# A decoder layer step on one core: stores a tile later, a strip loaded in four pieces and first, eight copies for sixteen, squares before a split

## What is computed

```python
q, k, v, u = mixer_inputs(rmsnorm(xp, norm_mix_g[l]), w_in[l])
att = dilated_attention_prompt(q, k, v, rpb_table)      # 12 heads of 64, causal, strided keys
u_full = jnp.pad(u, ((0, 0), (CONV_K - 1, 0), (0, 0)))
xp = xp + mixer_outputs(att, u_full, conv_w[l], conv_b[l], conv_ln_g[l], conv_ln_b[l], w_out[l])
...
xp = xp + cross_attend(rmsnorm(xp, norm_x_g[l]), mk, mv, w_xq[l], w_xo[l])
xp = xp + swiglu(rmsnorm(xp, norm_ffn_g[l]), w_ffn_gate[l], w_ffn_up[l], w_ffn_down[l])
...
kc = jnp.concatenate([cache_win_k[l].astype(k.dtype), k], axis=1)   # samples: 2048 cached + 8 new
s_wk.append(kc[:, -buf_len:])                                       # the cache moved on by 8 rows
```

## Time and profile before

| what | us |
|---|---|
| median of 3 runs | 1956.98 (1952.81 to 1958.29) |
| profiled execution, whole | 1964.15 |
| its span, first to last instruction | 1962.4 |
| TensorE busy | 1891.4 |
| DVE busy | 1030.5 |
| POOL busy | 513.6 |
| ACT busy | 442.4 |

### The profile page before, as it was taken

One profiled execution on the slowest core, in us unless ns is written; L12 is line 12 of the kernel. 1 busy time (PEld: TensorE's weight loads), 2 busy tenths in 40 slices (PEclk: granted clock), 3 DMA queues, 4 the chain that ended last, 5 costly groups with the idle time before them and its releaser, 6 DMA issues.

```text
span 1962.4 us, 33021 instructions
## 1 busy us (share of the span) xinstructions
PE 1891.4 (96%) x13253; PEld 1757.0 (90%) x13253; DVE 1030.5 (53%) x2099; ACT 442.4 (23%) x902; POOL 513.6 (26%) x380
## 2 busy tenths in 40 slices
PE   6999999999999899999999999999999999999998
PEld 6999888666666799999658999999999999999997
DVE  6698726666666553511653374544544544544544
ACT  5100013555545521200441031001001001001005
POOL 2332222000010135353001223222332222222234
PEclk9999999999999999899999999999999999999998
DMA  5399976686767512223630123432432432411102
GB/s 154 125 318 316 334 237 187 190 245 204 203 215 251 178 44 76 65 84 110 222 111 22 43 78 137 171 128 85 170 128 85 170 128 87 175 46 43 43 32 92
DMA packets 220002, 281.36 MB, mean 143 GB/s; under 512 B 7521, under 2 KB 206569, under 8 KB 218153
## 3 DMA queue, kind: packets, MB, share of 16 engines
q1 hardware_dynamic: 219901, 279.94, 43.8%
HBM read 266.48 MB, written 113.89 MB: 194 GB/s over the span
## 4 chain that ended last, share of the span: by engine, by line
PE 81%; DVE 8%; ACT 3%; SPq 3%; DMA 3%; issue 1%; POOL 1%; DVEq 0%; POOLq 0%; ACTq 0%
PE bank L1558 26%; PE bank L1594 13%; PE bank L1325 8%; PE bank L1086 7%; PE bank L1342 5%; PE bank L1033 3%; PE bank L1204 2%; DVE sp L2193 2%; PE bank L1305 2%; DMA w_raw<-in_w_in_dram 2%; SPq L651 2%; ACT p_T L1723 2%; PE bank L1177 2%; PE bank L1187 1%; PE bank L1520 1%; PE bank L1232 1%
## 5 line engine op out<-in xcount | busy, mean ns | idle before, releaser
L924 POOL CAST w_hi<-w_raw 128x1024 fp32r<-128x1024 f32 x98 | 105.1, 1073 | 967.7 <-issue 325.6
L1558 PE MATMUL bank<-g_lo,w_hi 128*128 128x362 f32 (+1 forms) x1008 | 334.0, 331 | 0.0
L1558 PE MATMUL bank<-g_hi,w_lo 128*128 128x362 f32 (+1 forms) x1008 | 333.6, 331 | 0.0
L1558 PE MATMUL bank<-g_hi,w_hi 128*128 128x362 f32 (+1 forms) x1008 | 331.0, 328 | 0.0
L926 POOL TENSOR_TENSOR w_lo<-w_raw,w_hi 128x1024 fp32r<-128x1024 f32 x98 | 248.2, 2533 | 7.8
L2599 DVE TENSOR_TENSOR xT<-bank,xT 128x362 f32<-128x362 f32 (+1 forms) x264 | 141.3, 535 | 121.7 <-PE bank L1594 121.7
L1558 PEld LDWEIGHTS bank<-g_hi,w_lo 128*128 128x128 f32 x1008 | 191.3, 190 | 0.0
L1558 PEld LDWEIGHTS bank<-g_hi,w_hi 128*128 128x128 f32 x1008 | 189.8, 188 | 0.3 <-POOL w_lo L926 0.3
L1558 PEld LDWEIGHTS bank<-g_lo,w_hi 128*128 128x128 f32 x1008 | 189.6, 188 | 0.0
L1594 PE MATMUL bank<-act_lo,w_hi 128*128 128x362 f32 (+1 forms) x480 | 157.5, 328 | 0.0
L1594 PE MATMUL bank<-act_hi,w_hi 128*128 128x362 f32 (+1 forms) x480 | 157.5, 328 | 0.0
(11 more groups left out here) (303 smaller groups left out, 3844.9 us busy)
## 6 DMA issues: line engine op xcount, KB each, us to landing
out_sk_dram<-in_cache_win_k_dram SPq DMA_DIRECT2D x24, 2040.0 KB
out_sv_dram<-in_cache_win_v_dram SPq DMA_DIRECT2D x24, 2040.0 KB
kb<-in_cache_win_k_dram SPq DMA_DIRECT2D x48, 512.0 KB, 5.0
vn<-in_cache_win_v_dram SPq DMA_DIRECT2D x22, 1024.0 KB, 8.2
w_raw<-in_w_in_dram SPq DMA_DIRECT2D x22, 512.0 KB, 11.9
w_raw<-in_w_ffn_gate_dram SPq DMA_DIRECT2D x22, 512.0 KB, 3.8
w_raw<-in_w_ffn_up_dram SPq DMA_DIRECT2D x22, 512.0 KB, 3.8
w_raw<-in_w_ffn_down_dram SPq DMA_DIRECT2D x22, 512.0 KB, 3.7
```

What stands on the lines that cost most here:

```text
L924: pool.tensor_copy(w_hi[slot][:, :], w_raw[slot][:, :]).then_inc(w_hi_done, 1)
L1558: last = pe.matmul(out, w, r, start=start, stop=stop)
```

## The change

Four parts, none of which changes what is computed.

1. In SP's loop the K of pair c is stored in the turn of tile 10 + 3c and V in that of tile 11 + 3c, a tile later than before. The store of K of pair 4 then comes behind the loop.
2. `d_strip` is loaded by four DMAs of 16 rows in place of eight of 8 rows. The first of these loads, with the wait for `d_made` ahead of it, is issued before `strip` and the last K store, not behind them.
3. `new_rows` fills `d_new` with eight copies, not sixteen: three units' columns are written by one copy from a broadcast source.
4. The last chunk's squares and their addition come ahead of the third group's `g_hi` and `g_lo`.

```diff
-                c, which = divmod(n - FIRST_QKV - 5, 3)
-                if n >= FIRST_QKV + 5 and which < 2:
+                c, which = divmod(n - FIRST_QKV - 6, 3)
+                if n >= FIRST_QKV + 6 and which < 2:
                     (store_k, store_v)[which](c)
                 for part in copies[:2]:
                     keep_rows(*part)
                 del copies[:2]
+            store_k(4)
...
             def load_sample_strip(p):
                 for g in range(4):
-                    for hh in range(2):
-                        row, head = 32 * g + NI * hh, 2 * member(4 * p, g)[0] + hh
-                        sp_.dma_start(d_strip[row:row + NI, :],
-                                      bass.AP(tensor=A["g_scratch"].tensor, offset=head * GL + ZERO - 7,
-                                              ap=[[1, NI], [1, BUF + NI]])).then_inc(d_loaded, 16)
+                    c = member(4 * p, g)[0]
+                    sp_.dma_start(d_strip[32 * g:32 * g + 2 * NI, :],
+                                  bass.AP(tensor=A["g_scratch"].tensor, offset=2 * c * GL + ZERO - 7,
+                                          ap=[[GL, 2], [1, NI], [1, BUF + NI]])).then_inc(d_loaded, 16)
...
             load_keys(0, 0)
+            sp_.wait_ge(d_made, 1)
+            load_sample_strip(0)
             load_strips(0)
             store_k(5)
-            sp_.wait_ge(d_made, 1)
-            load_sample_strip(0)
             sp_.wait_ge(k_out, 96)
...
-                pool.wait_ge(d_loaded, 128 * (p + 1))
+                pool.wait_ge(d_loaded, 64 * (p + 1))
...
                 act.wait_ge(r_added, 3 * KC + 3 + g + 1)
+                if g == 2:
+                    square(tools_x, 0, KC // 2 - 1, 1)
                 for k in range(KC):
                     act.activation(g_hi[:, k, t0:t0 + n], xT[:, k, t0:t0 + n], ACT.Copy,
                                    scale=gains[:, k:k + 1]).then_inc(n_hi, 1)
-            square(tools_x, 0, KC // 2 - 1, 1)
...
-                for e in range(4):
-                    for g in range(4):
-                        rows = slice(32 * g, 32 * g + 32)
-                        at = NI * member(e, g)[1]
-                        last = dve.tensor_copy(d_new[rows, e, at:at + NI], d_strip[rows, 7::-1])
+                first_three = d_new[:, :, :].rearrange("p e n -> p (e n)")[:, 0:3 * (TS + 16)]\
+                    .rearrange("p (e n) -> p e n", e=3)
+                for g in range(4):
+                    rows, at = slice(32 * g, 32 * g + 32), NI * member(0, g)[1]
+                    dve.tensor_copy(first_three[rows, :, at:at + NI],
+                                    d_strip[rows, 7::-1].unsqueeze(1).to_broadcast([32, 3, NI]))
+                    last = dve.tensor_copy(d_new[rows, 3, at + 48:at + 48 + NI], d_strip[rows, 7::-1])
...
                 add_out_group(KC - 1, g)
+                if g == 2:
+                    add_square(tools_x, 0, KC // 2 - 1, 1)
                 for k in range(KC):
                     dve.wait_ge(n_hi, KC * g + k + 1)
...
-            add_square(tools_x, 0, KC // 2 - 1, 1)
```

More of the change, by code:

```diff
@@ L2166, in new_rows @@
             def new_rows(p):
-                dve.wait_ge(d_loaded, 128 * (p + 1))
+                dve.wait_ge(d_loaded, 64 * (p + 1))
                 if p:
```

## The result

| | before | after |
|---|---|---|
| median of the runs, us | 1957.63 | 1975.80 |
| lowest and highest, us | 1952.68, 3062.97 | 1969.5, 1978.3 |
| profiled execution and its span, us | 1964.15, 1962.4 | 1977.48, 1975.7 |

One of the six executions of the kernel before took 3062.97 us, the next highest 1958.44, and one of the 23 beside the runs of single parts took 4234.32; neither is in a ratio.

What follows compares the result with a forecast made beforehand. TensorE, busy 1891.4 of 1962.4 us, was taken as the bound, so only its waits matter. Terms +11 (stores), -1.9 (strip), -3.3 (copies) and +0.2 (squares) sum to +6.0 on 1956.98: 1963.0 us, range 1953 to 1971.

Steps and rivals of the forecast that it cites:

- With 16 rows each the other half should work too: 3.4 us.: Attention's start: four 16-row loads would use all DMA engines, so the samples' strip takes 3.4 us, not 6.7.
- if the strip still takes 7 us: Attention's start: upper bound for the samples' strip change, +1.6 us, should its loading be no faster.
- a faster strip gives 1.9 us: Attention's start: second keys no longer share engines with the strip's end, land at 331.5, and TensorE starts 1.9 us earlier.
- The same DMAs end at the same time in either order: Projection stage: with a full queue, delayed K stores land when later loads did, by 229.18 and 276.85 us, 15 us later each.
- only the last stop counts, since it ends at a fixed time: Projection stage: TensorE's stop in tile 17 sets the cost; ACT's third copy at 277.7, not 263.64 us, +14.1 us.
- The half clock that was to follow that stop: Projection stage: 2.9 us lost after the new stop before tile 18, cancelling the 2.9 us lost before at tile 19.
- A: Rival, projection stage: K stores land nearly as before, TensorE loses only waits and half clock, 10.5 us; 1941.5 us, chance 0.08.
- B: Rival, projection stage: queue not strictly in order, K stores only about 7 us later; 1952.4 to 1955.3 us, chance 0.16.
- C: Rival, attention stage: strip no faster, second keys +1.6 us, copies of 24 columns take 0.27 us; 1967.3 us, chance 0.08.
- None for `w_lo` from tile 13 on: Sign, projection stage: TensorE would have no waits for these weights from tile 13 on, except at tile 15.
- The attention 10 us later: Sign: the attention stage would start some 10 us later in the profile after.
- TensorE's first wait for keys under 1 us: Sign, attention's start: TensorE's first wait for keys would fall from 2.54 us to under 1 us.

Runs made afterwards that it cites:

- p2_only: Kernel before with only the samples' strip changed: four loads of 16 rows, issued ahead of the strips and last K store; 1.0070, +13.7 us against the kernel before.
- p1_only: Kernel before with only the K and V stores of the projection stage a tile later; 1.0050, +9.8 us against the kernel before.
- k_twice: Kernel before with K and V stores a tile later and a second buffer for K (pairs 1 and 3); 0.9973, -5.3 us against the kernel before.
- lead16: Four strip loads ahead of the strips, each described with one leading dimension of 16 (second head's data wrong); 0.9999, -0.2 us against the kernel before.

## Why the prediction was wrong, by its own steps

**Part 2, the step that failed: "With 16 rows each the other half should work too: 3.4 us."** It scaled the share of the earlier trace rows with the number of rows. The number that counts is the leading dimension, 2 for the new loads: the strip took 12.4 us in the trace of after, on two engines. The term was -1.9 with an upper bound of +1.6 ("if the strip still takes 7 us"), and the part costs +13.7 (+10.0 to +17.6). Part 2 is 15.6 us over its term, more than the whole miss of 13.4; the other terms and the sum of the parts were 2.2 us too high together. The bound failed too: it took the old duration as the worst case, and that a form not in the trace may use fewer engines wasn't among the cases. The second omission is steps 8 and 16, where the same loads are issued again: the sum counted part 2 once, and TensorE waited 2.25 us at step 8 in p2_only as well. The third is the half clock behind the waits, 2.3 us more than in before by the count above. The step behind it, that a faster strip gives 1.9 us, stays open: with all 16 engines the strip took 5.2 us, not 3.4, and the run's -0.2 (-3.5 to +3.3) holds both 0 and -1.9. One reason to doubt it: the wait for keys of 2.54 us in the earlier trace rows, from which the term was made, is about 1 us or less in the traces of p1_only and k_twice, so this execution showed more to gain than there usually is.

**Part 1: right in the wait that costs; the size fits in part by luck, since two steps failed.** +11 forecast, +9.8 (+6.3 to +13.5) measured alone. Its inner steps fared unevenly. "The same DMAs end at the same time in either order" held to a few us: the stores landed at 227.0 and 272.4, with 229.18 and 276.85 taken. But "only the last stop counts, since it ends at a fixed time" failed. There was no stop in tile 17. The store had landed 4 us sooner than taken, and TensorE came there at about 275.4 (half a us ahead of ACT's third copy), not at 274. The third copy came at 275.91 for 263.64, +12.3 where +14.1 stood. The half clock that was to follow that stop didn't come either: the window 279 to 288 is at 1.00 for 0.62. So in the trace it is 12.3 - 3.8 - 2.9 = +5.6, near the +5.9 seen, where the prediction had +10.3. Some 2 us of the rest lie in the baseline: the kernels with its K stores usually reach the attention earlier than its profiled execution did (7.9 us between the means). The prediction had put this in its upper bound only. What is left, up to +9.8, is within the interval. A new wait of 1.91 us, for DVE's `half_vec`, was not foreseen; it is in all three traces with later K stores and one `k_nat`.

**Part 3: right.** -3.3 forecast, -3.1 (-5.5 to -0.8) measured alone. In the changed kernel its effect sits behind the new waits of part 2, but it is there: the parts add up.

**Part 4: not contradicted.** +0.2 forecast, 0.0 (-2.5 to +2.5) measured; a run can't tell the two apart.

**The rivals.** A lost to ACT's buffer, as argued against it; k_twice gives TensorE what A took for granted, no stop behind K, and it is worth -5.3 (-8.0 to -2.3), about half of A's -10.5. B's half delay isn't what happened. C had the right place, the samples' strip, and a reason in its last words (the rows lie in one group of partitions) that lead16 refutes. Its price of +1.6 was about a ninth of the real one. No case had part 2 above that, and so the range ended at 1971.

**The signs.** ACT's waits in tiles 11, 14 and 17: seen, the last until 272 us and not 277. Stops of TensorE before tiles 12 and 15 with the clock at half behind them: seen (3.6 and 7.0 us); before 18: not. None for `w_lo` from tile 13 on: true, even for all. The attention 10 us later: 5.9 in the trace. TensorE's first wait for keys under 1 us: wrong, 2.61 behind 4.25. The gap behind the copies at step 8 gone: seen.

## What to carry to other kernels

Before fewer and larger DMAs are costed, read the leading dimension of both sides of each. Here it went with the number of DMA engines (8, 2 and 16), and loads on two engines held up the strips, the store and the keys behind them. When stores are pushed behind loads, ask first who waits to reuse their buffer. Here a second buffer turned a loss of 9.8 us into a gain of 5.3. And a term built on a wait of one execution should be checked against how far that stage moves between executions.

## What the hardware showed unexpectedly

Two DMA engines moved 56 to 57 GB/s in the windows from 331 to 335 us, where eight moved 78: fewer engines were each faster, but not fast enough by far. A packet of the strip took 0.31 us at the median in the trace of after and 0.87 in that of before. Between executions of the kernel before and its near relatives the attention's start moved by 4.7 us (320.2 to 324.9), with the same instructions in the projection stage. Putting the samples' strip on 16 engines in place of 8 gave nothing that can be measured (-0.2 us at the front place, against +1.2 for the eight loads there, with intervals that overlap).
